# A state-space layer's skip, lows and carry moved between VectorE, TensorE, ScalarE and GpSimd

## The chip, the cores and the metric

One core of one Trainium2 chip runs the whole program in one launch. The metric is the device time of one execution in microseconds (us). Engines are named as in the profile: PE is TensorE's matmul side, PEld its weight loads, DVE is VectorE, ACT is ScalarE, POOL is GpSimd, SP issues the DMAs.

## The reference, cut to what matters

The program is two stacks of transformer-like layers over 256 tokens of width 1024. The change touches only the third layer of the first stack, a diagonal complex state space ("S5") with 64 groups of 64 states. With `u = xn @ w_in` it computes, in complex numbers, the recurrence `x[t] = a * x[t-1] + bbar @ u[t]`, and then

```
y = (einsum(c_re, xr) - einsum(c_im, xi))       # the outputs' sums
y = y.reshape(B, L, D_MODEL) + d_skip * u       # the skip
hg = gelu(y) @ w_glu
```

followed by a gated product and the residual. The layer is followed by a feed-forward layer and the rest of the program.

## The kernel before

All data are held feature-major: 128 partitions by 8 blocks of 256 tokens (`U5[:, k, :]` is `u` for block k). Weights stream from HBM in units of 1 MB into a ring of three; for every unit ACT makes the high part (L381, `whi`) and DVE the low part (L896, `wlo`), and PE multiplies high by high, high by low and low by high (L1683 to L1685). An operand has the same two parts: `XH` (ACT, counted by `op_hi`) and `XL` (DVE, counted by `op_lo`).

The order of work on each engine is written out by hand; every engine runs its own program in order and waits on semaphores. In the state space even and odd tokens are paired, so 128 pairs are scanned. They are cut in two halves of 64 (c = 0, 1) and the groups in four quarters (b = 0 to 3, called `qd` in places). That makes eight steps s = 2b + c. Steps of the two halves use two sets of four work buffers, `W5[s % 2]`. One step is:

- PE has written the inputs' sums of quarter b into banks 0 to 3 (L2206, `inputs(b)`, signalled by `bu_ready`).
- DVE, `products(s)`: four products of the sums in PSUM with tables in SBUF (L1317 to L1320), then an addition and a subtraction in SBUF (L1322, L1323).
- DVE, `scans(s)`: two scans (L1339, L1340). In the second half (c = 1) the state of the first half is first added in (L1337); it is computed after the first half's scans by four small products (L1346) and two small sums (L1353, L1354), on DVE ("jump"). Then two products turn the result back (L1348, L1349), signalled by `rot_ready`.
- POOL makes the two other products of the turn (L2406, L2407), signalled by `x5_ready`.
- PE, `outputs(s)`: 64 small fp32 products into bank 4 + b % 2 (L2235), signalled by `y5_ready`. With c = 0 the bank is zeroed first and a direct term is added (L2219, L2223). Between `outputs` PE computes one unit of an unrelated row of modulation vectors per step (L1697), and in odd steps the inputs of the next quarter ahead of it.
- DVE, `outputs(b)`: after both halves of quarter b, `u * d + sums` for its two blocks (L1362, `y5_sum`), put into DVE's queue after step 2b + 2. ACT then takes gelu (L664) and makes the high part (L666), and DVE makes the low part (`lows(b)`, L910), put after step 2b + 3.

After step 7 DVE makes the low part of a weight unit (L896), takes the sums of quarter 3 (L1362), copies the modulation rows (L984) and makes the last lows (L910). PE goes on with the gated product, whose first pass needs the lows of quarters 0 to 2 at once and those of quarter 3 after 18 matmuls.

A matmul of fp32 data stands in the trace as two records, a low-precision one as one.

Of the kernel before, what the change touches and what calls it, by code (L numbers as in the profile page):

```python
# [16 lines left out]
F32 = mybir.dt.float32  # L17
# [7 lines left out]
T = 256  # L25
# [43 lines left out]
def step5(s):  # L69

    return s % 2, s // 2
# [33 lines left out]
ITEMS, OUT0 = IN0 + 8, IN0 + 14  # L105

# [20 lines left out]
def program(nc, wst, mst, crow, vec, cst, xin, sgw, sgb, sbc, ctxin, ropes, out):  # L127
    with ExitStack() as ctx:
# [98 lines left out]
        def s5(i):  # L227
# [56 lines left out]
                 "v_ready", "scan_ready", "rot_ready", "x5_ready", "jump", "jump_parts", "y5_ready", "y5_sum",  # L284
                 "gelu5", "silu_c", "scp_nil", "mod_rows", "mod_sum", "mod_vec", "ctx_in", "mod_gain",
                 "c_in", "c_row", "ctx_rms", "ctx_inv", "ctx_diag", "ctx_row", "ml_in0", "ml_in1", "ml_used",
# [84 lines left out]
        def _(act):  # L371
# [275 lines left out]
            def state_space(i):  # L647
                scales()
                for n in range(4):
                    ahead(t.u)  # L650
                    t.u += 1
                    t.pp += 1
                    if n == 1:
                        turned(0)
                act.wait_ge(S["s5_k0"], 1)
                turned(1)
                act.activation(K0T, PS[:, 7, 0:256].rearrange("p (k n) -> p k n", n=32), ACT.Copy)\
                    .then_inc(S["s5_b"], 1)
                silu_c(1)
                t.u += MODS[0][1]  # L660
                for b in range(4):
                    act.wait_ge(S["y5_sum"], b + 1)
                    y = U5[:, 2 * b:2 * b + 2, :]
                    act.activation(y, y, ACT.Gelu_apprx_tanh).then_inc(S["gelu5"], 1)  # L664
                    act.wait_ge(S["gelu5"], b + 1)
                    act.activation(XH[:, 2 * b:2 * b + 2, T:2 * T], y, ACT.Copy).then_inc(S["op_hi"], 1)  # L666
                    if b == 2:
                        ahead(t.u)
                t.op += 4

                def ready(mp):
                    for j in (2 * mp, 2 * mp + 1):
                        ahead(t.u)
                        used(t.u)
                        act.activation(SG[:, j % 2, :], PS[:, 4 + t.pp % 2, T:2 * T], ACT.Sigmoid)\
                            .then_inc(S["glu_sig"], 1)
                        t.u += 1
                        t.pp += 1
                    act.wait_ge(S["glu_mul"], 2 * mp + 2)
                ahead(t.u)  # L680
                fresh(i, ready)
# [206 lines left out]
        def _(dve):  # L888
# [397 lines left out]
            def state_space(i):  # L1286
# [39 lines left out]
                def scans(s):  # L1326
# [16 lines left out]
                    if c == 0:  # L1343
                        zr, zi = (v.rearrange("p (a b) -> p a b", b=64)[:, :, 63] for v in (wk[1], wk[3]))
                        for o, x, y in ((JA, AR64, zr), (JB, AI64, zi), (JC, AR64, zi), (JD, AI64, zr)):
                            ins = dve.tensor_tensor(o[:, c8], x[:, c8], y, ALU.mult)  # L1346
                        ins.then_inc(S["jump_parts"], 1)
# [3 lines left out]
                    if c == 0:  # L1351
                        dve.wait_ge(S["jump_parts"], qd + 1)
                        dve.tensor_tensor(JRE[:, c8], JA[:, c8], JB[:, c8], ALU.subtract).then_inc(S["jump"], 1)  # L1353
                        dve.tensor_tensor(JIM[:, c8], JC[:, c8], JD[:, c8], ALU.add).then_inc(S["jump"], 1)  # L1354

                def outputs(b):

                    dve.wait_ge(S["y5_ready"], 2 * b + 2)
                    for kk in range(2):
                        u5 = U5[:, 2 * b + kk, :].rearrange("p (c e) -> p c e", e=2)  # L1360
                        y5 = PS[:, 4 + b % 2, kk * T:(kk + 1) * T].rearrange("p (e c) -> p c e", e=2)
                        ins = dve.scalar_tensor_tensor(u5, u5, vcol("ssm_d", 2 * b + kk), y5, ALU.mult, ALU.add)  # L1362
                    ins.then_inc(S["y5_sum"], 1)

                def lows(b):
                    low(XL[:, 2 * b:2 * b + 2, T:2 * T], U5[:, 2 * b:2 * b + 2, :], XH[:, 2 * b:2 * b + 2, T:2 * T],
                        t.op + b + 1)

                for s in range(8):
                    products(s)  # L1370
                    scans(s)
                    if s >= 2:
                        (lows if s % 2 else outputs)(s // 2 - 1)
                split_lo(t.s)
                t.s += 1
                outputs(3)
# [300 lines left out]
        def _(pe):  # L1677
# [505 lines left out]
            def state_space():  # L2183
# [26 lines left out]
                def outputs(s):  # L2210
# [5 lines left out]
                    if c == 0:  # L2216
                        if b >= 2:
                            pe.wait_ge(S["y5_sum"], b - 1)
                        pe.matmul(bank, ZB[:, 0:P], ZB[:, :], start=True, stop=False, **kw)  # L2219
                        for kk in range(2):  # L2220
                            for q in range(4):
                                r = slice(32 * q, 32 * q + 32)
                                pe.matmul(bank[r, kk * T:kk * T + P], K0T[r, 2 * b + kk, :], U5[r, 2 * b + kk, 0:T:2],  # L2223
                                          start=False, stop=False, **kw)
                    pe.wait_ge(S["rot_ready"], s + 1)
# [46 lines left out]
        def _(pool):  # L2272
# [127 lines left out]
            for s in range(8):  # L2400

                (c, qd), wk = step5(s), W5[s % 2]
                tc, ts = (AR[:, B0 + o + 512 * qd:B0 + o + 512 * qd + 512] for o in (12288, 10240))

                pool.wait_ge(S["rot_ready"], s + 1)
                pool.tensor_tensor(wk[1], wk[1], ts, ALU.mult)  # L2406
                pool.tensor_tensor(wk[3], wk[3], tc, ALU.mult).then_inc(S["x5_ready"], 1)  # L2407
# [109 lines left out]
```

## Time and profile before

| | us |
|---|---|
| three runs, median (lowest, highest) | 1827.54 (1827.36, 1828.07) |
| the profiled execution, its own time | 1829.06 |
| its span, first to last instruction | 1827.2 |
| PE busy | 1708.1 (93%) |
| DVE busy | 1248.8 (68%) |
| ACT busy | 844.6 (46%) |
| POOL busy | 163.0 (9%) |

The span is the time from the first to the last instruction; the execution's own time holds what lies around it. Busy time says how long an engine had an instruction in work. Start times below are counted from the span's start; the eight steps run from about 684 us to 759 us.

### The profile page before, as it was taken

To read this page: it belongs to the slowest core of one execution; us is meant where nothing else is said; L and a number is where in the kernel's file an instruction comes from. 1 tells how busy PE (TensorE), PEld (TensorE's weight loads), DVE (VectorE), ACT (ScalarE), POOL (GpSimd) and SP (SyncE) were. 2 spreads that over 40 slices of the span, in tenths; PEclk is the share of its full clock that TensorE was granted. 3 is DMA by queue.
4 is the path that set the end of the run, shared out by engine and by line. 5 is a ranking of instruction groups with operands and counts; after the bars stand their busy time and mean duration, and the time that the engine had idled before them with its cause. 6 is when DMAs were issued, how large, how long until landed. Compare 5 with 4: busy or idle time off the path is not lost.

```text
span 1827.2 us, 34733 instructions
## 1 busy us (share of the span) xinstructions
PE 1708.1 (93%) x14503; PEld 1616.3 (88%) x14514; DVE 1248.8 (68%) x1580; ACT 844.6 (46%) x962; POOL 163.0 (9%) x130
## 2 busy tenths in 40 slices
PE   6999999889899997799999999999979899999997
PEld 6979999889899985699999988999978579889997
DVE  5847777786877759767777774777774575664444
ACT  5355554546455530355545445555554533143333
POOL 1002000104910062200000101000000000000000
PEclk9999999999999999999999999999989999899999
DMA  7904545544455423444555761454432121035551
GB/s 299 333 1 162 190 178 184 184 162 152 150 181 184 164 91 117 163 162 162 182 184 181 270 252 47 179 191 168 183 111 93 69 93 70 24 138 184 184 184 69
DMA packets 40050, 286.50 MB, mean 157 GB/s; under 512 B 4576, under 2 KB 4576, under 8 KB 5664
## 3 DMA queue, kind: packets, MB, share of 16 engines
q1 hardware_dynamic: 39024, 280.99, 42.8%
q10 hardware_dynamic: 944, 4.33, 0.7%
q8 instruction: 63, 1.03, 0.2%
q14 instruction: 19, 0.16, 0.0%
HBM read 284.25 MB, written 1.05 MB: 156 GB/s over the span
## 4 chain that ended last, share of the span: by engine, by line
PE 64%; DVE 17%; ACT 9%; issue 6%; POOL 2%; DMA 1%; DVEq 0%; ACTq 0%; POOLq 0%; SPq 0%
PE PS L1683 19%; PE PS L1684 18%; PE PS L1685 18%; ACT whi L381 4%; DVE wlo L896 4%; DVE AR L1082 4%; ACT AR L486 1%; POOL AR L2389 1%; PE PS L1779 1%; DVE AR L1193 1%; DVE XL L940 1%; DVE AR L1190 1%; ACT AR L576 1%; ACT AR L578 1%; PE PS L2235 1%
## 5 line engine op out<-in xcount | busy, mean ns | idle before, releaser
L1683 PE MATMUL PS<-XH,whi 128*128 128x256 f32 (+1 forms) x2696 | 788.8, 293 | 45.0 <-DVE wlo L896 23.8
L1684 PE MATMUL PS<-XL,whi 128*128 128x256 f32 (+1 forms) x2696 | 780.2, 289 | 0.0
L1685 PE MATMUL PS<-XH,wlo 128*128 128x256 f32 (+1 forms) x2696 | 780.1, 289 | 0.0
L896 DVE TENSOR_TENSOR wlo<-raw,whi 128x2048 fp32r<-128x2048 f32 x240 | 558.9, 2331 | 187.7 <-ACT whi L381 187.6
L1683 PEld LDWEIGHTS PS<-XH,whi 128*128 128x128 f32 x2696 | 523.6, 194 | 58.1 <-issue 34.0
L1684 PEld LDWEIGHTS PS<-XL,whi 128*128 128x128 f32 x2696 | 524.1, 194 | 4.4 <-issue 0.2
L1685 PEld LDWEIGHTS PS<-XH,wlo 128*128 128x128 f32 x2696 | 523.7, 194 | 4.1
L381 ACT ACTIVATE whi<-raw 128x2048 fp32r<-128x2048 f32 x240 | 456.0, 1902 | 72.8 <-PE PS L1685 48.4
L1683 PE MATMUL PS<-HH,whi 128*128 128x256 f32 x880 | 251.8, 286 | 13.0 <-DVE HL L1102 8.5
L1685 PE MATMUL PS<-HH,wlo 128*128 128x256 f32 x880 | 251.0, 285 | 0.0
L1684 PE MATMUL PS<-HL,whi 128*128 128x256 f32 x880 | 250.8, 285 | 0.0
L1683 PEld LDWEIGHTS PS<-HH,whi 128*128 128x128 f32 x880 | 170.7, 194 | 14.8 <-DVE HL L1102 9.5
L1082 DVE SCALAR_TENSOR_TENSOR AR<-AR,VEC 128x255 f32<-128x255 f32 (+1 forms) x352 | 161.7, 501 | 15.4 <-ACT AR L486 4.7
L1684 PEld LDWEIGHTS PS<-HL,whi 128*128 128x128 f32 x880 | 170.6, 194 | 0.0
L1685 PEld LDWEIGHTS PS<-HH,wlo 128*128 128x128 f32 x880 | 170.5, 194 | 0.0
L489 ACT ACTIVATE AR<-AR 128x256 f32<-128x256 f32 x88 | 36.7, 418 | 268.4 <-DVE AR L1082 268.4
L2389 POOL TENSOR_TENSOR AR<-AR 128x512 f32<-128x512 f32 x24 | 56.0, 2335 | 916.3 <-ACT AR L435 916.2
L486 ACT ACTIVATE AR<-AR,VEC 128x256 f32<-128x256 f32 x176 | 95.6, 590 | 86.1 <-DVE AR L1068 86.1
L1068 DVE TENSOR_TENSOR AR<-PS,SM 128x512 f32<-128x512 f32 x88 | 60.7, 689 | 27.2 <-PE PS L1685 24.1
L1683 PE MATMUL PS<-whi,XH 128*128 128x256 f32 x256 | 74.1, 289 | 2.5 <-DVE XL L940 2.5
L1684 PE MATMUL PS<-wlo,XH 128*128 128x256 f32 x256 | 73.3, 286 | 0.0
L1685 PE MATMUL PS<-whi,XL 128*128 128x256 f32 x256 | 73.2, 286 | 0.0
(336 smaller groups left out, 1583.7 us busy)
## 6 DMA issues: line engine op xcount, KB each, us to landing
raw<-wst SPq DMA_DIRECT2D x248, 1024.0 KB, 4.8
AR<-mst SPq DMA_DIRECT2D x17, 1024.0 KB, 6.2
XT<-x_in SPq DMA_DIRECT2D x2, 512.0 KB, 6.0
AR<-crow ACTq DMA_DIRECT2D x2, 512.0 KB, 5.8
AR<-sbc ACTq DMA_DIRECT2D x1, 1024.0 KB, 6.6
AR<-ctxin ACTq DMA_DIRECT2D x1, 1024.0 KB, 5.8
y_out<-XT SPq DMA_DIRECT2D x1, 1024.0 KB, 3.9
AR<-sgw ACTq DMA_DIRECT2D x1, 512.0 KB, 3.7
```

The source lines that it names most:

```text
L381: act.activation(whi[:, r, :], raw[:, u % RING, :], ACT.Copy).then_inc(S["w_hi"], 1)
L486: a = act.activation(CA[:, j % 2, i, :], UA[:, j % 2, i, :], ACT.Identity, bias=cb, scale=w2)
L489: act.activation(SG[:, j % 2, :], CA[:, j % 2, 1, :], ACT.Silu).then_inc(S["silu_ready"], 1)
L576: act.activation(EX[:, p % 2, :], ZC[:, p % 2, :], ACT.Exp).then_inc(S["ex_ready"], 1)
L578: act.activation(LN[:, p % 2, :], EX[:, p % 2, :], ACT.Ln, bias=1.0)\
L896: dve.tensor_tensor(wlo[:, r, :], raw[:, u % RING, :], whi[:, r, :].bitcast(F32), ALU.subtract)\
L1068: dve.tensor_tensor(UA[:, j % 2], bank, RSTD.unsqueeze(1).broadcast_to([P, 2, T]), ALU.mult)\
L1082: ins = dve.scalar_tensor_tensor(y, UA[:, j % 2, i, 0:T - back], w, y, ALU.mult, ALU.add)
L1683: pe.matmul(dst, sh, mh, start=first, stop=False, **kw)
L1684: pe.matmul(dst, sh, ml, start=False, stop=False, **kw)
L1685: return pe.matmul(dst, sl, mh, start=False, stop=last, **kw)
L2389: ins = pool.tensor_tensor(SQ[:, 0:2, :], SQ[:, 0:2, :], SQ[:, 2 * mp:2 * mp + 2, :], ALU.add)
```

## The change

Four pieces of work of the eight steps move. (1) The skip: POOL multiplies `U5` by `d_skip` in place, two instructions per quarter, after the first half's `outputs` have been computed (`u5_skip`); PE adds the result into the bank with two fp32 matmuls by the identity, just ahead of the second half's `outputs`; DVE's L1362 is gone. (2) ACT takes its gelu straight from the PSUM bank when `y5_ready` says that both halves are there, and writes it to `U5`; the bank is released by `gelu5`. (3) The lows of quarters 0 to 2 are made by POOL; those of quarter 3 stay on DVE. (4) The four small products and two small sums that carry the state from the first half to the second are made by POOL, ahead of its two products of the turn.

```
 # ACT
-                    act.wait_ge(S["y5_sum"], b + 1)
+                    act.wait_ge(S["y5_ready"], 2 * b + 2)
                     y = U5[:, 2 * b:2 * b + 2, :]
-                    act.activation(y, y, ACT.Gelu_apprx_tanh).then_inc(S["gelu5"], 1)
+                    act.activation(y.rearrange("p k (c e) -> p k c e", e=2),
+                                   PS[:, 4 + b % 2, :].rearrange("p (k e c) -> p k c e", k=2, e=2), ACT.Gelu_apprx_tanh)\
+                        .then_inc(S["gelu5"], 1)
 # DVE, scans(s)
-                    if c == 0:
-                        zr, zi = (v.rearrange("p (a b) -> p a b", b=64)[:, :, 63] for v in (wk[1], wk[3]))
-                        for o, x, y in ((JA, AR64, zr), (JB, AI64, zi), (JC, AR64, zi), (JD, AI64, zr)):
-                            ins = dve.tensor_tensor(o[:, c8], x[:, c8], y, ALU.mult)
-                        ins.then_inc(S["jump_parts"], 1)
...
-                    if c == 0:
-                        dve.wait_ge(S["jump_parts"], qd + 1)
-                        dve.tensor_tensor(JRE[:, c8], JA[:, c8], JB[:, c8], ALU.subtract).then_inc(S["jump"], 1)
-                        dve.tensor_tensor(JIM[:, c8], JC[:, c8], JD[:, c8], ALU.add).then_inc(S["jump"], 1)
-
-                def outputs(b):
-
-                    dve.wait_ge(S["y5_ready"], 2 * b + 2)
-                    for kk in range(2):
...
-                        ins = dve.scalar_tensor_tensor(u5, u5, vcol("ssm_d", 2 * b + kk), y5, ALU.mult, ALU.add)
-                    ins.then_inc(S["y5_sum"], 1)
 
                 def lows(b):
+                    dve.wait_ge(S["op_lo"], t.op + b)
...
                 for s in range(8):
                     products(s)
                     scans(s)
-                    if s >= 2:
-                        (lows if s % 2 else outputs)(s // 2 - 1)
                 split_lo(t.s)
                 t.s += 1
-                outputs(3)
+                dve.wait_ge(S["y5_ready"], 8)
 # PE, outputs(s)
                         if b >= 2:
-                            pe.wait_ge(S["y5_sum"], b - 1)
+                            pe.wait_ge(S["gelu5"], b - 1)
...
+                    if c:
+                        pe.wait_ge(S["u5_skip"], b + 1)
+                        for kk in range(2):
+                            pe.matmul(bank[:, kk * T:(kk + 1) * T], ident,
+                                      U5[:, 2 * b + kk, :].rearrange("p (c e) -> p e c", e=2), start=False, stop=False, **kw)
                     pe.wait_ge(S["rot_ready"], s + 1)
 # POOL
+                for s in range(8):
+                    (c, qd), wk = step5(s), W5[s % 2]
...
+                    if c == 0:
+                        pool.wait_ge(S["scan_ready"], s + 1)
+                        zr, zi = (v.rearrange("p (a b) -> p a b", b=64)[:, :, 63] for v in (wk[1], wk[3]))
+                        for o, x, y in ((JA, AR64, zr), (JB, AI64, zi), (JC, AR64, zi), (JD, AI64, zr)):
+                            ins = pool.tensor_tensor(o[:, c8], x[:, c8], y, ALU.mult)
+                        ins.then_inc(S["jump_parts"], 1)
+                        pool.wait_ge(S["jump_parts"], qd + 1)
+                        pool.tensor_tensor(JRE[:, c8], JA[:, c8], JB[:, c8], ALU.subtract).then_inc(S["jump"], 1)
+                        pool.tensor_tensor(JIM[:, c8], JC[:, c8], JD[:, c8], ALU.add).then_inc(S["jump"], 1)
+                    pool.wait_ge(S["rot_ready"], s + 1)
+                    pool.tensor_tensor(wk[1], wk[1], ts, ALU.mult)
+                    pool.tensor_tensor(wk[3], wk[3], tc, ALU.mult).then_inc(S["x5_ready"], 1)
+                    b = s // 2
+                    if s % 2 == 0 and s:
+                        pool.wait_ge(S["op_hi"], OP5 + b)
+                        k = slice(2 * b - 2, 2 * b)
+                        pool.tensor_tensor(XL[:, k, T:2 * T], U5[:, k, :], XH[:, k, T:2 * T].bitcast(F32), ALU.subtract)\
+                            .then_inc(S["op_lo"], 1)
+                    if s % 2 == 0:
+                        pool.wait_ge(S["y5_ready"], s + 1)
+                        for kk in range(2):
+                            u5 = U5[:, 2 * b + kk, :]
+                            ins = pool.tensor_scalar(u5, u5, vcol("ssm_d", 2 * b + kk), None, ALU.mult)
+                        ins.then_inc(S["u5_skip"], 1)
```

## Rows read from the trace of the kernel before

**Rows 1.** Chain in order of time (start us, us, what): one round of two steps
```profile
699.95 0.69 DVE AR L1317
...
706.17 0.42 DVE SM L1346 x4
...
713.19 2.21 issue
```

**Rows 2.** Timeline of DVE (start us, us, instruction, [idle before <-releaser]), steps 2 to 4
```profile
706.51 0.68 DVE L1348 TENSOR_TENSOR AR<-AR 128x512 f32<-128x512 f32 x1
...
707.71 0.16 DVE L1353 TENSOR_TENSOR SM<-SM 128x8 f32<-128x8 f32 x1
...
707.86 0.87 DVE L1362 SCALAR_TENSOR_TENSOR AR<-AR,VEC,PS 128x256 f32<-128x256 f32 x2
...
708.65 0.68 DVE L1317 TENSOR_TENSOR AR<-PS,AR 128x512 f32<-128x512 f32 x1
...
711.16 0.69 DVE L1322 TENSOR_TENSOR AR<-AR 128x512 f32<-128x512 f32 x1
...
716.36 0.68 DVE L910 TENSOR_TENSOR XL<-AR,XH 128x512 fp32r<-128x512 f32 x1
717.40 0.69 DVE L1317 TENSOR_TENSOR AR<-PS,AR 128x512 f32<-128x512 f32 x1 [0.36 <-PE PS L2206]
```

**Rows 3.** Timeline of POOL, step 2
```profile
707.87 1.27 POOL L2406 TENSOR_TENSOR AR<-AR 128x512 f32<-128x512 f32 x1 [5.62 <-DVE AR L1349]
709.10 1.27 POOL L2407 TENSOR_TENSOR AR<-AR 128x512 f32<-128x512 f32 x1
```

**Rows 4.** Timeline of PE, from the inputs of quarter 2 to outputs(4)
```profile
717.29 2.99 PE L1697 MATMUL PS<-raw,SM 128*32 128x256 f32 x13
...
726.33 0.66 PE L2223 MATMUL PS<-AR,VEC 32*32 32x128 f32 x16 [0.25 <-DVE AR L1362]
727.97 1.99 PE L2235 MATMUL PS<-AR 128*32 128x64 f32 x128 [0.98 <-POOL AR L2407]
```

**Rows 5.** Timeline, POOL and DVE side by side, in the layer before
```profile
456.24 1.90 POOL L2304 COPY AR<-AR 128x2048 f32<-128x2048 f32 x1
```

**Rows 6.** Timeline of DVE in the layer before: L1102 beside L2304, and alone
```profile
456.78 1.90 DVE L1102 TENSOR_TENSOR HL<-AR,HH 128x512 fp32r<-128x512 f32 x1 [0.70 <-ACT HH L502]
...
474.89 0.73 DVE L1102 TENSOR_TENSOR HL<-AR,HH 128x512 fp32r<-128x512 f32 x1
```

**Rows 7.** Timeline behind step 7: POOL's turn beside DVE's weight lows, and outputs(7)
```profile
751.26 1.64 POOL L2406 TENSOR_TENSOR AR<-AR 128x512 f32<-128x512 f32 x1 [6.13 <-DVE AR L1349]
751.70 3.35 DVE L896 TENSOR_TENSOR wlo<-raw,whi 128x2048 fp32r<-128x2048 f32 x1
752.86 3.31 POOL L2407 TENSOR_TENSOR AR<-AR 128x512 f32<-128x512 f32 x1
...
756.32 3.15 PE L2235 MATMUL PS<-AR 128*32 128x64 f32 x128 [5.60 <-POOL AR L2407]
...
759.54 0.87 DVE L1362 SCALAR_TENSOR_TENSOR AR<-AR,VEC,PS 128x256 f32<-128x256 f32 x2 [4.49 <-PE PS L2235]
```

**Rows 8.** Timeline of POOL before the steps: prices of its operations
```profile
443.40 0.26 POOL L2296 TENSOR_TENSOR AR<-AR 128x32 f32<-128x32 f32 x1
...
674.47 0.60 POOL L2382 COPY AR<-AR 64x512 f32<-64x512 f32 x1
675.05 1.49 POOL L2383 TENSOR_SCALAR AR<-AR 64x512 f32<-64x512 f32 x1
```

**Rows 9.** Groups of instructions, PE: fp32 products with 256 moving columns
```profile
L1883 PE MATMUL PS<-AR,CST 128*128 128x256 f32 x32 | 11.4, 440 | 4.0 <-DVE AR L1193 3.8
```

**Rows 10.** Stretches: us, busy PE, PEld, DVE, ACT, POOL (count), PEclk, DMA share, GB/s
```profile
700.00:717.40 17.40, 13.93 (x369) 9.64 (x369) 16.80 (x31) 1.26 (x2) 5.63 (x5) 1.00 0.37 124
751.20:762.50 11.30, 5.49 (x146) 5.23 (x146) 6.05 (x7) 3.92 (x4) 4.92 (x2) 0.85 0.53 187
```

**Rows 11.** Timeline of PE: the gated product waits for the last lows
```profile
762.52 0.39 PE L1683 MATMUL PS<-XH,whi 128*128 128x256 f32 x1 [0.71 <-DVE XL L910]
```

More of the change, by code:

```diff
@@ L105 @@
 ITEMS, OUT0 = IN0 + 8, IN0 + 14
+OP5 = 6 * KT + 4
 class Tally:
@@ L283, in program @@
                  "s5_angle", "s5_table", "s5_xb", "s5_turned", "s5_b", "bu_ready", "bu_mult",
-                 "v_ready", "scan_ready", "rot_ready", "x5_ready", "jump", "jump_parts", "y5_ready", "y5_sum",
+                 "v_ready", "scan_ready", "rot_ready", "x5_ready", "jump", "jump_parts", "y5_ready",
                  "gelu5", "silu_c", "scp_nil", "mod_rows", "mod_sum", "mod_vec", "ctx_in", "mod_gain",
-                 "c_in", "c_row", "ctx_rms", "ctx_inv", "ctx_diag", "ctx_row", "ml_in0", "ml_in1", "ml_used",
+                 "c_in", "c_row", "u5_skip", "ctx_rms", "ctx_inv", "ctx_diag", "ctx_row", "ml_in0", "ml_in1", "ml_used",
                  "normed", "wide_taken", "csq", "csum", "crms", "crinv", "cnormed", "kv_part", "q_out", "rot",
@@ L1350, in scans @@
                         .then_inc(S["rot_ready"], 1)
-                    if c == 0:
-                        dve.wait_ge(S["jump_parts"], qd + 1)
-                        dve.tensor_tensor(JRE[:, c8], JA[:, c8], JB[:, c8], ALU.subtract).then_inc(S["jump"], 1)
-                        dve.tensor_tensor(JIM[:, c8], JC[:, c8], JD[:, c8], ALU.add).then_inc(S["jump"], 1)
-                def outputs(b):
-                    dve.wait_ge(S["y5_ready"], 2 * b + 2)
-                    for kk in range(2):
-                        u5 = U5[:, 2 * b + kk, :].rearrange("p (c e) -> p c e", e=2)
-                        y5 = PS[:, 4 + b % 2, kk * T:(kk + 1) * T].rearrange("p (e c) -> p c e", e=2)
-                        ins = dve.scalar_tensor_tensor(u5, u5, vcol("ssm_d", 2 * b + kk), y5, ALU.mult, ALU.add)
-                    ins.then_inc(S["y5_sum"], 1)
                 def lows(b):
+                    dve.wait_ge(S["op_lo"], t.op + b)
                     low(XL[:, 2 * b:2 * b + 2, T:2 * T], U5[:, 2 * b:2 * b + 2, :], XH[:, 2 * b:2 * b + 2, T:2 * T],
@@ L2399, in _, with turns @@
             shifted_outputs()
[L2400 to L2407, printed above, removed]
+            def turns():
+                for s in range(8):
+                    (c, qd), wk = step5(s), W5[s % 2]
+                    c8 = slice(8 * qd, 8 * qd + 8)
+                    tc, ts = (AR[:, B0 + o + 512 * qd:B0 + o + 512 * qd + 512] for o in (12288, 10240))
+                    if c == 0:
[22 more added lines that the diff above has]
+                        ins.then_inc(S["u5_skip"], 1)
@@ L2408, in _ @@
+            turns()
             for n in range(5, 8):
```

## The prediction

> **What bounds the kernel now.** I read the table of busy times first: PE is busy for 93% of the span, so a layer costs time mainly where PE stands still, and the eight steps of the state space are such a place. The stretches [rows 10] say who is full there: of 17.40 us DVE is busy 16.80, PE 13.93, POOL 5.63. Then the chain in order of time [rows 1], for one round of two steps: from step 2's first product (699.95) to step 4's (717.40, [rows 2]) is 17.45 us. It runs DVE (products, scans, the carry's small products L1346, turn), POOL (two products, 707.87 to 710.37 [rows 3]), PE's outputs, and the next quarter's inputs, with 2.21 us in the middle in which PE waits for nothing that the profile shows. The timeline of DVE [rows 2] shows that this is not alone: DVE's own work of the round fills all but 0.36 us before 717.40. And PE has 0.98 us left in a round [rows 4]. So three loops of nearly one length run side by side: DVE 17.1, POOL with PE 17.45, PE's own work some 16.5. Shortening one gives only the distance to the next. Last I read what follows step 7 [rows 7, 11].
>
> **What DVE loses in work.** Start to start in [rows 1, 2]: the four small products 0.34 (706.17 to 706.51), the two small sums 0.15 (707.71 to 707.86), the skip 0.79 (707.86 to 708.65), the lows 0.60 (0.68 long, the next starts 0.08 before its end). That is 1.88 a round: an even step is 7.91 - 0.49 = 7.42, an odd one stays at 7.71 (708.65 to 716.36), together 15.13. The 0.34 also lies on the chain through POOL.
>
> **What POOL gains, and its prices.** Six small products or sums of 128x8, one low part of 128x512, two scalings of 128x256. Small: 128x32 takes 0.26 and 128x512 takes 1.27 [rows 3, 8], so 2.1 ns an element and 0.20 for 8 elements, 0.16 start to start; bounds 0.15 and the 0.34 that a chained one needs with its wait (0.26 and 0.08 of handing on). Low part: 1.27, the same form as L2406. Scaling: the same operation on 512 elements of 64 partitions takes 1.49, a copy of that size 0.60 [rows 8]; half of each and a little start gives 0.8 and 0.4. I take 0.8, since the operation is the same, and keep both ends.
>
> **They exclude each other.** This decides the case. L2407 beside the weight lows L896 takes 3.31 instead of 1.27 [rows 3, 7]: L2406 ends at 752.90, L896 ends 2.15 later, L2407 1.12 after that. So L896 stood behind L2406 and L2407 behind L896. In [rows 5, 6] L2304 ends at 458.14 and L1102, 0.73 alone, ends at 458.68 after 1.90. Each time one ends its own length less 0.15 after the other's end, and they take turns. Beside products that read PSUM there is no such thing: L2406 and L2407 take 1.27 beside L1317 of step 3 [rows 2, 3]. Today POOL works almost only there. The new work doesn't: the small products start with DVE's turn (L1348), the low part and the scalings fall beside L1322, L1323, L1337 and the scans, all of them with two inputs in SBUF.
>
> The Trainium skill, SBUF — State Buffer, section Who interferes with whom, says the same as a rule: a VectorE instruction with two SBUF inputs contends with a GpSimd one that reads SBUF, whoever issues first gets the pair for the whole instruction, and the other fully blocks. The trace agrees for L896 and L1102; for the scans, which also have two, no run here shows it. By the rule they take part; without them the sum would be about 1.5 us less.
>
> **The round, with turns.** Let R be the end of DVE's turn in an even step. Two of the six small ones get between L1348 and L1349 and just behind; four are left, with a wait of POOL for its own count, so L2406 starts at R + 0.77 instead of R + 0.08. The chain through POOL becomes 17.45 - 0.34 + 0.69 = 17.8. L2407 ends at R + 3.27. DVE comes to L1322 at R + 2.44, so it ends 0.68 late; POOL's low part has the next turn, L1323 ends 1.05 late (its shift by 0.68 not counted again); PE's outputs end near R + 5.6 and the two scalings of 0.8 come beside L1337 and the scans, 0.6 each. Sum 2.93. DVE's loop is 15.13 + 2.93 = 18.06, the longest of the three: +0.61 against 17.45. So the work taken off DVE comes back as waiting, and a little more.
>
> **The skip on PE.** Two fp32 products by the identity: 32 records of mostly this form take 11.4 us busy [rows 9], 0.36 each, so about 0.71 a product as an upper bound; two records of 0.23 (13 of L1697 in 2.99, [rows 4]) give 0.46 as the lower. PE's own round is 6.8 (707.87 + 2.64 to 717.29) and 9.7 (717.29 to 726.99), 16.5; with 0.9 to 1.4 it is 17.4 to 17.9, under 18.06: hidden. Were DVE not the longest, PE would be. Its wait for `u5_skip` has the outputs and everything of PE behind it, but the scalings end some 5 us before PE gets there. The wait for `gelu5` in place of `y5_sum` is for a bank freed a round earlier: nothing.
>
> **Sum up to step 7.** Step 0 and 1: no low part, but L1322 is late by 0.68 and the scalings meet the turn of step 1, 1.04: +1.72 - 0.49, less a wait for PE that goes (I take the 0.36 of step 4) = +0.87. Steps 2 and 3: +0.61. From 717.40 to R of step 7, 751.18 ([rows 7], L2406's start less 0.08), it is 33.78 now; then 18.06 + 7.42 + 7.79 + 2.93 = 36.20: +2.42. This last is most of it, since no chain through PE stands beside DVE in steps 6 and 7. Together +3.9.
>
> **Behind step 7.** Now 751.18 to 756.17 for POOL's two products. Then DVE, rid of the low part, starts L896 (2.30 alone by [rows 7]) before POOL wakes: 2.22 + 1.12 + 1.23 = 4.57, -0.42. Next, outputs(7) takes 3.15 where the same takes 1.99 at full clock [rows 4, 7]: PE stood still for 5.60 us before and the granted clock of that stretch is 0.85 [rows 10]; PE will stand still nearly as long, so I keep it. ACT then starts on PSUM itself: L1362's 0.87 and its handing on go. But PE waits only 0.71 for the last lows [rows 11], behind 18 matmuls that it can do anyway, so that is all it gets: -0.71. Gelu from PSUM in another order may be slower than 0.63; this has 0.2 us of cover. Everything behind is bound by PE and shifts along.
>
> Total +3.9 - 0.42 - 0.71 = +2.8. The profiled execution, 1829.06 (span 1827.2), becomes 1831.8; the runs lie 1.5 below it, so 1827.54 + 2.8 = 1830.3, 0.15% more. What this kernel's measurement can tell from no change is about 0.2%, 3.7 us: 1823.9 to 1831.2.
>
> **Rivals.**
> (A) POOL's new work costs DVE nothing, because the scans don't take part and the short pieces slip into gaps. For it: small instructions, off DVE's queue, and DVE idles between its own waits. Against it: [rows 5 to 7]. Then PE's own work bounds the rounds (-0.2 up to step 6), steps 6 and 7 give DVE's 0.49 and 0.79, and the end 0.42 and 0.71: -2.6, 1824.9; with scalings and clock kinder still, 1823.5.
> (B) Slower: POOL's small work between scans and turn. If each of the six costs 0.34 instead of 0.16, L2406 starts 0.9 later still, all that follows on POOL meets more of DVE's scans, and four even steps pay 0.6 to 0.7 more each: 1830.3 + 2.8 = 1833.1. It decides from about 0.25 a piece. For it: every chained small one of the setup needs 0.34 with its wait, and the reads of the state have a stride of 64 elements, which no row shows. Against it: only one of six waits here.
> (C) PE is kept awake by the skip's products before outputs(7), which then takes 2.0: 1.2 less than the forecast, 1829.1. Against it: PE still stands still some 5 us.
> (D) Scalings cheap (0.4) and scans free of turns: the chain through POOL binds at +0.35 a round, and the end takes most of it back: 1827.8. The Trainium skill, GPSIMD Engine Reference, section 4.1 Engine selection, calls one-input work there roughly line-rate, which speaks for the cheap end, about 2 us less than my sum; the 1.49 of [rows 8] speaks against it.
>
> **Numbers.** Forecast 0.45, B 0.25, D 0.12, A 0.12, C 0.06. The forecast's own spread is 1.5 us, so a quarter of it is above 1831.2, with nine tenths of B: slower 0.34. Faster is the better half of A and what I haven't thought of: 0.10. The rest, 0.56, is no change. The range is 1824.8 (A's) to 1833.8 (a little over B's).
>
> **What would show it.** Right: L1322 of the odd steps at 1.3 to 1.4 us, L1323 at 1.7, scans of the odd steps at 1.8; POOL's low part at 1.7; L1322 to L1323 of even steps unchanged at 0.69; R of step 7 some 4 us later; the start of the gated product's seventh block 2 to 3 us later than 762.52 with no wait. Wrong: scans at 1.22 and 1.20 beside POOL's scalings (then D or A), R of step 7 earlier than 751.18 (A), small products at 0.3 (B), outputs(7) at 2 us (C), or PE's stall of 2.2 us in a round going away or coming twice, which would move a round by as much.

## The result and the profile after

| | before | after |
|---|---|---|
| median of 8 runs each (lowest, highest), us | 1827.45 (1825.42, 1830.30) | 1832.01 (1830.73, 1836.68) |
| the profiled execution: its own time, span | 1829.06, 1827.2 | 1831.81, 1829.7 |
| busy PE, DVE, ACT, POOL | 1708.1, 1248.8, 844.6, 163.0 | 1713.5, 1248.5, 844.6, 183.7 |
| steps: first product of step 0 to the gated product's first matmul | 683.96 to 759.40, 75.44 | 684.28 to 766.66, 82.38 |

The ratio after to before is 1.0033 [1.0021, 1.0044]: 0.33%, or 4.6 us in medians. That is slower by more than the 0.2% that this kernel's measurement can tell. The forecast was 1830.3 in a range of 1824.8 to 1833.8.

The steps cost 6.9 us more, the profiled span only 2.5. Up to the gated product everything is late by 7.26; the rest of the program, in which nothing was changed, took 4.8 us less in this pair of profiles, which hold one execution of each kernel. The section on the prediction comes back to it.

The busy times of the page after, against the table of before:

```profile
span 1829.7 us, 34778 instructions
...
PE 1713.5 (94%) x14530; PEld 1615.5 (88%) x14530; DVE 1248.5 (68%) x1545; ACT 844.6 (46%) x962; POOL 183.7 (10%) x165
```

DVE has lost 35 instructions (1580 before) and is busy as long as before: what it waits for within an instruction counts as busy. Its timeline after (start us, us, instruction, [idle before <-releaser]), step 3 and the start of step 4, to hold against [rows 2]:

```profile
708.50 0.68 DVE L1320 TENSOR_TENSOR AR<-PS,AR 128x512 f32<-128x512 f32 x1
...
711.01 1.42 DVE L1325 TENSOR_TENSOR AR<-AR 128x512 f32<-128x512 f32 x1
712.36 1.76 DVE L1326 TENSOR_TENSOR AR<-AR 128x512 f32<-128x512 f32 x1
...
714.43 1.22 DVE L1342 TENSOR_TENSOR_SCAN AR<-AR 128x512 f32<-128x512 f32 x1
715.58 1.35 DVE L1343 TENSOR_TENSOR_SCAN AR<-AR 128x512 f32<-128x512 f32 x1
716.96 0.78 DVE L1346 TENSOR_TENSOR AR<-AR 128x512 f32<-128x512 f32 x1
...
720.39 0.69 DVE L1320 TENSOR_TENSOR AR<-PS,AR 128x512 f32<-128x512 f32 x1 [2.04 <-PE PS L2190]
...
740.86 0.69 DVE L1320 TENSOR_TENSOR AR<-PS,AR 128x512 f32<-128x512 f32 x1 [3.10 <-PE PS L2190]
```

The addition and the subtraction (L1325, L1326; they were L1322 and L1323) take 1.42 and 1.76 instead of 0.69 and 0.68. And then DVE stands idle for 2.04 and 3.10 us until PE has the next inputs; before, that was 0.36 [rows 2]. The timeline of POOL after, same stretch, to hold against [rows 3]:

```profile
707.32 1.66 POOL L2399 TENSOR_TENSOR SM<-SM,AR 128x8 f32<-128x8 f32 x4 [3.60 <-DVE AR L1343]
...
709.39 1.28 POOL L2405 TENSOR_TENSOR AR<-AR 128x512 f32<-128x512 f32 x1
710.61 1.28 POOL L2406 TENSOR_TENSOR AR<-AR 128x512 f32<-128x512 f32 x1
711.84 1.73 POOL L2411 TENSOR_TENSOR XL<-AR,XH 128x512 fp32r<-128x512 f32 x1
714.40 3.25 POOL L2417 TENSOR_SCALAR AR<-AR,VEC 128x256 f32<-128x256 f32 x2 [0.83 <-PE PS L2224]
```

The low part (L2411) takes 1.73, and the two scalings 3.25 together beside the scans. The timeline of PE after, from step 2's modulation product to step 4's, answers to [rows 1, 4]:

```profile
707.21 3.62 PE L1681 MATMUL PS<-raw,SM 128*32 128x256 f32 x16
...
712.03 2.26 PE L2224 MATMUL PS<-AR 128*32 128x64 f32 x128 [0.30 <-POOL AR L2406]
714.22 0.49 PE L2190 MATMUL PS<-AR 32*128 32x128 f32 x3
717.69 2.65 PE L2190 MATMUL PS<-AR 32*128 32x128 f32 x61 [2.98 <-issue]
720.27 4.69 PE L1681 MATMUL PS<-raw,SM 128*32 128x256 f32 x16
724.89 1.17 PE L2212 MATMUL PS<-AR,CST 128*128 128x256 f32 x4
725.99 1.98 PE L2224 MATMUL PS<-AR 128*32 128x64 f32 x128
...
738.40 2.42 PE L2190 MATMUL PS<-AR 32*128 32x128 f32 x51 [3.49 <-issue]
```

Three things are to be seen. PE's wait for POOL ahead of outputs(2) has shrunk from about 1 us to 0.30. The gap inside the inputs (L2190; L2206 before), in which PE waits for nothing that the profile names, has grown from 2.21 to 2.98 and from 2.17 to 3.49. And behind it the same 16 records of modulation take 4.69 instead of 3.62. The stretches after (us, busy PE, PEld, DVE, ACT, POOL, PEclk, DMA share, GB/s) show the granted clock, against [rows 10]:

```profile
701.00:720.30 19.30, 16.02 (x374) 10.76 (x373) 17.11 (x22) 1.23 (x2) 14.01 (x16) 0.97 0.33 112
720.30:740.80 20.50, 17.01 (x376) 11.13 (x375) 16.93 (x22) 1.23 (x2) 11.99 (x14) 0.92 0.30 105
```

It was 1.00 in the round of before [rows 10]; after, it stands at the lower of its two levels (1.2 GHz instead of 2.4) for 3.4 us from 719.0 and again from 739.5, each time behind the long gap. PE's timeline of before has, for the second of its gaps:

```profile
733.02 1.63 PE L2206 MATMUL PS<-AR 32*128 32x128 f32 x43 [2.17 <-issue]
```

By rounds (first product of steps 0, 2, 4, 6, and the end of DVE's turn in step 7) it was 15.99, 17.45, 17.28, 16.49 before and is 16.59, 19.52, 20.47, 17.38 after. So the question of the experiments was what sets the two rounds of about 20 us: DVE's turn-taking with POOL, or PE's gap.

### The profile page after: what moved, and what is told of

The parts are those of the page before. It is cut to its first block, busy times and chain, and to the rows that moved or that the text cites. A ratio compares the mean times of both kernels' runs of the same rounds, so it can differ in the third digit from the quotient of the medians.

```text
span 1829.7 us, 34778 instructions
## 1 busy us (share of the span) xinstructions
PE 1713.5 (94%) x14530; PEld 1615.5 (88%) x14530; DVE 1248.5 (68%) x1545; ACT 844.6 (46%) x962; POOL 183.7 (10%) x165
## 4 chain that ended last, share of the span: by engine, by line
PE 66%; DVE 16%; ACT 9%; issue 6%; POOL 2%; DMA 1%; DVEq 0%; ACTq 0%; POOLq 0%; SPq 0%
PE PS L1667 19%; PE PS L1669 19%; PE PS L1668 19%; ACT whi L382 4%; DVE wlo L899 4%; DVE AR L1085 4%; ACT AR L487 1%; POOL AR L2378 1%; PE PS L2224 1%; PE PS L1763 1%; DVE AR L1196 1%; DVE AR L1193 1%; PE PS L1681 1%; ACT AR L577 1%; ACT AR L579 1%
```

## The experiments

Eleven kernels were run, in three groups, each beside the kernel before on its own chip (medians of before 1827.88, 1826.78 and 1827.95). "Steps" is the stretch of the table above; the gaps are the two inside PE's inputs; "rest" is from the gated product's start to the start of the last low part of a weight. Steps, gaps and rest are read from one profile of each kernel.

| kernel | median us | ratio to before | steps | gaps | rest |
|---|---|---|---|---|---|
| before | | 1 | 75.44 | 2.21, 2.17 | 1049.57 |
| after | 1832.01 | 1.0033 [1.0021, 1.0044] | 82.38 | 2.98, 3.49 | 1044.72 |
| e1_skip_only | 1833.42 | 1.0033 [1.0021, 1.0044] | 80.85 | 3.25, 3.52 | 1047.56 |
| e2_skip_back | 1828.92 | 1.0009 [0.9999, 1.0018] | 76.10 | 1.66, 1.80 | 1048.39 |
| e3_before_pad | 1830.87 | 1.0017 [1.0008, 1.0027] | 77.61 | see below | 1046.42 |
| e4_after_pad | 1835.34 | 1.0039 [1.0025, 1.0054] | 80.58 | see below | 1048.53 |
| e5_after_late | 1828.49 | 1.0008 [0.9999, 1.0018] | 78.12 | 1.06, 0.94 | 1044.70 |
| e6_after_split | 1835.60 | 1.0043 [1.0026, 1.0059] | 85.30 | 2.98, 3.41 | 1047.78 |
| e7_before_split | 1829.08 | 1.0011 [1.0001, 1.0021] | 79.35 | 2.48, 2.28 | 1047.74 |
| e8_act_split | 1832.49 | 1.0031 [1.0021, 1.0041] | 83.74 | 2.98, 2.78 | 1046.66 |
| e9_act_late | 1828.29 | 0.9996 [0.9986, 1.0006] | 74.14 | 1.48, 0.95 | 1048.13 |
| e10_before_late | 1824.87 | 0.9986 [0.9977, 0.9995] | 75.45 | 1.11, 0.83 | 1046.76 |
| e11_skip_late | 1825.13 | 0.9989 [0.9979, 0.9998] | 74.59 | 1.06, 1.16 | 1045.46 |

**First group: which part costs, and does the gap belong to a place in the program?**

e1_skip_only keeps the skip (parts 1 and 2) and puts the carry and the lows back on DVE:

```
+                    if c == 0:      # DVE, scans(s)
+                            ins = dve.tensor_tensor(o[:, c8], x[:, c8], y, ALU.mult)
...
+                    if s % 2 and s >= 3:
+                        lows(s // 2 - 1)
```

> Only the skip's part of the change: GpSimd scales, PE adds through the identity, ScalarE takes gelu from PSUM. The carry (four products, two sums) and all lows are on VectorE as before. Two theories. (P) PE's own loop has become the longest: the identity's products cost it 1.1 us a round and the gap inside the inputs (L2206) is longer than 2.2 us, because PE now comes to the burst without waiting. Then the rounds stay at 19 to 20 us, the steps (first product of step 0 to the first matmul of the gated product, 75.4 us before, 82.4 after) take 80 to 83, VectorE waits 2 us or more for L2206 in steps 4 and 6, and the time is 4 to 6 us over the kernel before. (T) The turns that VectorE and GpSimd take on each other (L1325 1.41, L1326 1.76 in the changed kernel) are the cost: then with no low part and no carry on GpSimd most of it goes, the steps take 75 to 77 us and the time is within 1 us of the kernel before.

Measured: the whole loss is there with the skip alone, 1.0033. PE's timeline shows the long gap and the slow stretch behind it, and DVE, whose work of a round is less than before by the skip, waits 2.81 and 3.88 us for the inputs:

```profile
717.76 2.89 PE L2200 MATMUL PS<-AR 32*128 32x128 f32 x61 [3.25 <-issue]
720.58 4.44 PE L1691 MATMUL PS<-raw,SM 128*32 128x256 f32 x16
724.95 1.17 PE L2222 MATMUL PS<-AR,CST 128*128 128x256 f32 x4
```

The second gap is 3.52. So PE's side sets the rounds, not the turn-taking.

e2_skip_back is the other half: carry and lows on POOL, the skip back on DVE, and gelu behind it as before.

```
+                        ins = dve.scalar_tensor_tensor(u5, u5, vcol("ssm_d", 2 * b + kk), y5, ALU.mult, ALU.add)
+                    ins.then_inc(S["y5_sum"], 1)
```

> The other half alone: the carry and the lows of quarters 0 to 2 stay on GpSimd, the skip is VectorE's sum as before, no identity products, no scaling, gelu from SBUF. (P): PE's program in the steps is that of the kernel before, so its gap stays at 2.2 us and its loop at some 17.3; VectorE's loop is 15.9 plus turns of 0.7 and 1.1, 17.7; the steps take 76 to 78 us and the time is 0 to 2 us over the kernel before. (T): the turns are the cost and are all here except the scalings': the steps take 80 us or more, the time 3 us or more over the kernel before.

Measured: 1.0009 [0.9999, 1.0018], steps +0.7. PE waits 1.4 us for POOL ahead of the even outputs, and the gaps are down to 1.66 and 1.80, where I had expected them to stay at 2.2. Waits and gap go against each other: outputs that start later come nearer to the moment at which the gap ends anyway.

e3_before_pad and e4_after_pad put products on 32x32 zeros into PE's program, without any use for them, so that new blocks of PE's program begin at other places in the work:

```
+                for _ in range(69):     # ahead of the steps; 65 in e4
+                    pe.matmul(PS[0:32, 6, 0:32], ZB[0:32, 0:32], ZB[0:32, 0:32], start=True, stop=True)
...
+                    for _ in range(59 if s == 7 else 0):     # 63 in e4
```

> The kernel before with 69 tiny padding products (138 instructions of PE) put where PE waits ahead of step 0, and 59 more where it waits ahead of outputs(7), 256 instructions in all, so that the program behind keeps its place in 16 KB blocks. If the gap of 2.2 us inside the inputs of quarters 2 and 3 is PE waiting for the next block of its program (16384-byte packets on the instruction queue start at 712.95 and 730.59, within 0.3 us of both gaps), the gap moves out of the inputs by 118 to 146 instructions, to the modulation products behind them or to another burst, and the rounds become VectorE's 17.1: the steps 0.5 to 1 us shorter. If the gap has to do with the data or the semaphores of the inputs it stays at the same matmul and nothing changes.

> The changed kernel with 65 such padding products ahead of step 0 and 63 ahead of outputs(7). (P) with the gap as a wait for the program: the gaps of 2.98 and 3.49 us leave the inputs, PE's loop falls from 19.5 and 20.5 to some 17, VectorE's loop with its turns (15.1 plus 2.1, 17.2) becomes the longest: the steps take 76 to 78 us instead of 82.4, the time comes back to within 1.5 us of the kernel before. (T): the turns don't change, so the steps stay above 80 us.

Both missed in time: the steps were 2.2 longer in e3 than in before and only 1.8 shorter in e4 than in after, and neither kernel was faster than the one it was made from. The 80.58 of e4 even lies where the rival (T) had it; the steps alone would not have told the two apart. What they did show is where the gap went. PE's timeline of e3:

```profile
722.80 1.77 PE L2235 MATMUL PS<-AR 128*32 128x64 f32 x113 [1.05 <-POOL AR L2411]
728.65 0.65 PE L2235 MATMUL PS<-AR 128*32 128x64 f32 x15 [4.09 <-issue]
```

and of e4:

```profile
723.91 1.75 PE L2224 MATMUL PS<-AR 128*32 128x64 f32 x109
729.85 0.74 PE L2224 MATMUL PS<-AR 128*32 128x63 f32 x18 [4.20 <-issue]
```

The gap has left the inputs and stands within outputs(3), and is longer: 4.09 and 4.20. It follows the position in PE's program and not the work, which speaks for the fetch of the program. In the packets of e3 the weight load lies at 722.89 to 726.48 and the program's packet starts at 726.44; in e4 the load ends at 727.55 and the packet starts at 727.55. That gave the next theory: the block is fetched only when the weight load that is under way ends.

**Second group: the load in the way of the block.** In the kernel before, the DMA rows of 709.50 to 712.90 show the 1 MB load alone on queue q1:

```profile
DMA packets 132, 1.05 MB, mean 308 GB/s; under 512 B 4, under 2 KB 4, under 8 KB 4
...
q1 hardware_dynamic: 132, 1.05, 88.2%
```

and those of 709.50 to 713.90 have one packet more of queue q8, 16 KB of instructions, which starts at 712.95:

```profile
DMA packets 145, 1.07 MB, mean 242 GB/s; under 512 B 16, under 2 KB 16, under 8 KB 16
...
q1 hardware_dynamic: 144, 1.05, 68.3%
q8 instruction: 1, 0.02, 1.3%
```

After, the load lies at 711.97 to 715.44 and 732.56 to 736.09, and the packets start at 715.44 and 736.09. The load is issued 1.15 us behind the even step's modulation product, which frees its buffer. So from the end of that product to PE's going on there is a nearly fixed time: 708.60 to 715.40 and 726.08 to 733.02 before, 710.83 to 717.69 and 731.42 to 738.40 after; 6.80, 6.94, 6.86, 6.98. In e1 it is 6.89 and 7.00, in e2 6.60 and 6.97. It is the 1.15 to the load, 3.4 to 3.5 of the load, and 2.25 to 2.45 from the packet's start to PE's next matmul.

The Trainium skill, Runtime: NRT & Kernel Launch, section Instruction fetch mechanics, says that an engine's program comes in blocks of 256 instructions while the present one runs, and that crossing a boundary is mostly hidden. The blocks agree with the 16 KB packets here; the hiding does not: PE stands for 1.7 to 4.2 us in the kernels up to e4.

e5_after_late changes nothing but the time of two loads: in `load` SP also waits until PE has the inputs of the round. (For this SP's loop over these loads is written out, as it is in e6 to e11 too.)

```
                 sp.wait_ge(S["w_used"], before + 1 + step)
+                if before - MODS[0][0] in (2, 4):
+                    sp.wait_ge(S["bu_ready"], (before - MODS[0][0]) // 2 + 2)
```

> The changed kernel, PE's program untouched; only SP issues two of the weight loads later: those that fill the place of the modulation units 2 and 4 also wait until the inputs of quarters 2 and 3 are computed. New theory (Q): in every run so far the program block that PE lacks in its gap starts on the DMA engines exactly when the 1 MB weight load ends (before: loads end at 713.15 and 730.71, blocks start at 712.95 and 730.59; changed: 715.44 and 736.09, blocks at 715.44 and 736.09), and PE goes on 2.3 us later. The load starts 1.15 us after the modulation product of an even step, so the inputs end at a fixed time after that product and PE's 1 us of waiting ahead of outputs(2) was never to spare. With the loads out of the way the block comes within a few tenths of PE's reaching the one before: the gaps inside the inputs (2.98, 3.49) fall under 0.7 us, the rounds from 19.5 and 20.5 to 17.2 to 18.5, and a shorter gap may come in the outputs of steps 3 and 5, beside the moved loads. Rival (R): the gap is the time that a block always takes, the load only happens to end then: gaps and rounds stay.

Measured: steps 78.12 instead of 82.38, 1.0008 instead of 1.0033. With no load near (the loads lie at 706.81 to 710.36 and 720.21 to 727.20), the DMA rows of 710.80 to 715.80 hold the block alone, at 714.71:

```profile
DMA packets 1, 0.02 MB, mean 3 GB/s; under 512 B 0, under 2 KB 0, under 8 KB 0
...
q8 instruction: 1, 0.02, 1.3%
```

and the timeline of PE has short gaps and no slow stretch behind them:

```profile
717.06 2.09 PE L2192 MATMUL PS<-AR 32*128 32x128 f32 x61 [1.06 <-issue]
719.08 3.64 PE L1683 MATMUL PS<-raw,SM 128*32 128x256 f32 x16
...
734.24 1.85 PE L2192 MATMUL PS<-AR 32*128 32x128 f32 x51 [0.94 <-issue]
```

DVE's turn-taking is untouched by this, as its timeline says:

```profile
712.28 1.42 DVE L1327 TENSOR_TENSOR AR<-AR 128x512 f32<-128x512 f32 x1
713.62 1.76 DVE L1328 TENSOR_TENSOR AR<-AR 128x512 f32<-128x512 f32 x1
```

With no load near, the packet starts 1.41 us behind the first product of outputs(2) and again of outputs(4) (713.30 and 730.52 in e5); in after it was 3.41 and 3.83, in before 2.43 and 2.62. This settles the cause of the long rounds: the load delays the block, and the delay closes PE's loop. The gaps stayed a little over the 0.7 that I had expected. The rounds from steps 2 and 4 fell from 19.52 and 20.47 to 17.23 and 17.35; the first round is longer than in after, 17.75 instead of 16.59, with the granted clock at the lower level for 10.2 us from 691.2 instead of 6.8 from 691.7.

e6_after_split and e7_before_split cut these loads into four of 256 KB, so that the block could come between them:

```
+                    for c0 in range(512, UNIT, 512):
+                        sp.dma_start(raw[:, u % RING, c0 - 512:c0], wst[u][:, c0 - 512:c0]).then_inc(S[f"piece{u % RING}"], 16)
```

> The changed kernel with each of the five weight loads between two modulation units issued as four DMAs of 256 KB (512 columns each) instead of one of 1 MB. (Q), if the block waits in its DMA engines for the rest of one transfer: it gets in between the pieces, the gaps shrink by some 2 us to about 1, rounds 17.5 to 18.5, steps 77 to 79 us. If it waits for all that is queued, split or not, the gaps stay at 3.0 and 3.5 and so does the time.

> The kernel before with the same split loads. (Q): its gaps of 2.21 and 2.17 go or shrink below 1; the chain through PE gets shorter than VectorE's own loop of 17.1, so the rounds fall only from 17.45 and 17.28 to 17.1: 0.5 us in all, not to be seen in the time.

Missed. The pieces of the loads between two steps together take 5.4 to 5.9 us in e6 instead of 3.45. The block does start within the load there (716.82, in a load of 713.41 to 718.88, and 737.43, in one of 733.59 to 739.49), but not sooner: 3.37 and 3.85 us behind the first product of the outputs, with whole loads 3.41 and 3.83. The gaps are 2.98 and 3.41, and in e7 2.48 and 2.28. Both kernels have SP's loop written out and still have the gaps, so it was not this that shortened them in e5. PE's timeline of e6 has the slow stretch in the inputs themselves, 3.42 for 61 records:

```profile
719.15 3.42 PE L2197 MATMUL PS<-AR 32*128 32x128 f32 x61 [2.98 <-issue]
```

e8_act_split has the split loads, carry and lows on DVE, and the scaling on ACT instead of POOL:

```
+                        a = act.activation(u5, u5, ACT.Copy, scale=vcol("ssm_d", 2 * b + kk))
+                    a.then_inc(S["u5_skip"], 1)
```

> A version that should beat both if (Q) holds: the skip through the identity with its scaling on ScalarE instead of GpSimd (so GpSimd and VectorE never meet), gelu from PSUM, carry and lows on VectorE as before, split loads. VectorE's loop is 17.1 less 0.8 for the skip's sums, 16.3; PE's 16.5 less 2.2 for the gap plus 1.1 for the identity, 15.4; through GpSimd 17.45 less 2.2. Rounds of 16.3 to 16.6, steps 72 to 73 us against 75.4 before, time 2 to 4 us under the kernel before. If splitting doesn't shorten the gap, PE's loop of 19.5 stays and it is as slow as the skip alone, 80.9 us of steps.

Missed too, and twice: the gaps are 2.98 and 2.78 and the rounds from steps 2 and 4 20.02 and 19.06; and there is a new wait in quarter 3, where the scaling stands in ACT's queue behind the high parts of weights. PE's timeline:

```profile
761.66 2.07 PE L2234 MATMUL PS<-AR,CST 128*128 128x256 f32 x4 [7.64 <-ACT AR L671]
```

**Third group: late loads in every version.** e9 is e8 with the loads whole and late, e10 the kernel before with late loads, e11 the skip alone (e1) with them. Each has the lines of e5:

```
+                if before - MODS[0][0] in (2, 4):
+                    sp.wait_ge(S["bu_ready"], (before - MODS[0][0]) // 2 + 2)
```

> The version that both findings point to: the skip through the identity, scaled on ScalarE (quarter 3's scaling ahead of the weight highs that come between gelu 2 and 3), gelu from PSUM, carry and lows on VectorE, and the two weight loads held until the inputs are computed. (Q): gaps of about 1 us or less, no turns on VectorE; VectorE's loop 16.3, PE's 16.5 - 2.2 + 1.0 + 1.1 = 16.4; rounds of 16.3 to 16.7, steps 72.5 to 74 us against 75.4 before, time 1.5 to 3 us under the kernel before (ratio 0.9985 to 0.999). (T), turns alone matter: also good, since there are none. (R), the gap doesn't depend on the load: rounds stay at 19.

> The kernel before with the two held loads alone. (Q): the gaps of 2.21 and 2.17 fall to 1 or less, but VectorE's own loop of 17.1 takes over at once: rounds 17.1 to 17.2, the time within 1 us of the kernel before. So what e9 gains over this is the skip's.

> The skip alone with its scaling on GpSimd (as in the changed kernel), carry and lows on VectorE, held loads. Against e9 it shows what the scalings' turns cost: VectorE's loop 16.2 plus 0.3 for scans and turn that start late, so rounds of 16.4 to 16.8; against the skip alone with early loads (rounds 19.8 and 20.5, 1.0033) it shows what the load costs: some 3 us a round. Time within 1 us of e9. If GpSimd's scalings push its own products of the odd step late, up to 17.2.

e9 can't be told from before; e10 and e11 are below it, by 0.14% [0.05, 0.23] and 0.11% [0.02, 0.21], less than the 0.2% that I called the bound. They beat both kernels of the case in their medians, though little, and are not to be told from each other. The gaps and rounds came out nearly as expected (16.3 to 16.8 in e9, 16.5 and 16.8 in e11, 17.0 in e10), the times did not: e9 gained nothing of its 1.5 to 3 us, and e10, which was to gain at most 1, gained most. PE's timeline of e11 shows the round without its stall:

```profile
715.85 2.09 PE L2202 MATMUL PS<-AR 32*128 32x128 f32 x61 [1.06 <-issue]
...
732.62 1.85 PE L2202 MATMUL PS<-AR 32*128 32x128 f32 x51 [1.16 <-issue]
```

Two differences can be read from the group. e1 to e11, with the skip: holding the loads takes 6.3 us off the steps. e11 to e5, both with late loads: the steps with carry and lows on POOL are 78.12 - 74.59 = 3.5 us longer, but 1.5 of that lies in the first round, where the clock of e5 was lower for longer; the other rounds are longer by 0.5, 0.8 and 1.5, and what follows step 7 is 0.7 shorter. Here DVE is the longest again, and the turn-taking is what one pays. In e10 the steps are as long as before (75.45) although both gaps halved, because PE now waits for POOL instead (1.64 us ahead of outputs(4)); its gain in the median lies outside the steps, and its cause was not settled:

```profile
715.86 1.96 PE L2208 MATMUL PS<-AR 32*128 32x128 f32 x57 [1.11 <-issue]
729.13 2.03 PE L2237 MATMUL PS<-AR 128*32 128x64 f32 x128 [1.64 <-POOL AR L2409]
```

So of what e5 and e11 gain in time over after and e1, up to some 2.6 us may be this same gain and not the shorter gaps; no run has SP's loop written out with nothing else changed.

## Why the prediction was right or wrong

The direction was right and the time within 1.7 us, but the class was not: I gave "no change" 0.56 and it is slower. And the mechanism was half of the real one; that the time came so near is in part luck, since the stretch with the change lost more than twice the forecast and the rest of the program, which the forecast left as it was, took less. Up to the gated product's seventh block I forecast +2.8; it starts at 769.22 instead of 762.52 [rows 11], +6.4 us when the start of step 0 (+0.3) is taken off. The rounds say where the 3.6 us of error are: steps 0 and 1 +0.60 (forecast +0.87), steps 2 and 3 +2.07 (+0.61), from there to the end of step 7's turn 37.85 instead of 33.77, +4.08 (+2.42), and behind that -0.37 (-1.13).

**The step that failed** is "The skip on PE", where it said "PE's own round is 6.8 ... and 9.7 ..., 16.5; with 0.9 to 1.4 it is 17.4 to 17.9, under 18.06: hidden". The working counted PE's 0.98 us ahead of outputs(4) [rows 4] as slack. It was none: the gap in the inputs ends about 6.9 us behind the even step's modulation product, whatever outputs do in between; outputs that start earlier only lengthen the gap. PE's loop was already 17.6 us (715.40 to 733.02: 10.7 of work from the inputs' going on to the end of the modulation product, 6.9 behind it), as long as the round. What is added to the 10.7 is added to the round: the identity products 1.10 (inside my 0.9 to 1.4), and, since the gap then grows and the clock falls behind it, 1.07 on L1681 and 0.6 on the inputs. 17.6 + 2.8 = 20.4, and the round from step 4 is 20.47; the one from step 2, in which the first long gap falls and whose start it doesn't yet set, is 19.52. I had listed the stall as something that might go or come twice; I had not asked what it hung on. e1, e5 and e11 together show this.

**Turn-taking on DVE.** Right in kind, and well in size for the additions: L1325 1.42 and L1326 1.76 (forecast 1.3 to 1.4 and 1.7), the low part 1.73 (1.7), POOL's turn 0.81 behind the end of DVE's (0.77). The Trainium skill's rule (SBUF — State Buffer, section Who interferes with whom), that the one who is behind fully blocks, agrees with the 1.42 and 1.76. Wrong for the scans: 1.22 and 1.35 where I had 1.8 each. There POOL waits, 3.25 for two scalings that take 0.93 each with nothing of DVE beside them (e4, at 739.43), and the scan hardly does. The first scaling starts at 714.40, the scan at 714.43; by that rule, in which the first one keeps the shared pair for its whole instruction, the scan should have waited as the additions did, and the measurement decides. DVE's cost of a round was thus 0.73 + 1.08 + 0.15 + 0.09 = 2.05 and not 2.93 (in step 5 it is 1.85). In the kernel as it was changed this is hidden, since DVE is idle for 2.04 and 3.10 us behind it; with the loads held it is part of what e5 has over e11.

**Small operations on POOL.** Forecast 0.20 each, measured 0.20 (L2402, L2403). Rival B, which had 0.34 for them, came out at nearly the right time (1833.1) for a wrong reason.

**Behind step 7.** POOL's two products 4.54 us by the forecast 4.57, right. The timeline of POOL after, against [rows 7]:

```profile
758.32 3.24 POOL L2405 TENSOR_TENSOR AR<-AR 128x512 f32<-128x512 f32 x1 [0.78 <-DVE AR L1347]
761.52 1.26 POOL L2406 TENSOR_TENSOR AR<-AR 128x512 f32<-128x512 f32 x1
```

The last lows are no longer waited for, as said (-0.71). But outputs(7) takes 3.81, not the 3.15 that I kept: the term is short by 0.66. The granted clock is at its lower level from 763.4 to 766.8, nearly all of outputs(7); before, it was from 755.4 to 758.8, with outputs(7) from 756.32 to 759.47.

**Rivals.** A (no cost on DVE) fell with L1325 and L1326. D was half right: the scans are nearly free of turns, 1.22 and 1.35, but the scalings are not cheap, 0.93 alone where D has 0.4 and the forecast 0.8, and its 1827.8 is missed by 4.2 because PE's loop binds. C (outputs(7) at 2 us) fell with its 3.81. The true rival, PE's loop as the longest, stands in the working as one clause without a price of its own.

**What the rest gave back.** Behind the steps the same code took 1044.72 instead of 1049.57. The clock's records there show 37.7 us at the lower level after and 47.8 before; over the thirteen kernels that time lies between 37.7 and 53.4 and the rest between 1044.7 and 1049.6. The shortest rests (after, e5, e11) have the least of it (37.7, 37.7, 41.9), but beyond these the order is loose: e2, with the most, is 1.2 us shorter than before. That the clock makes these differences is not shown, and one profile stands for each kernel. In medians the loss is 4.6 of the 6.9 us.

## What to carry to other kernels

A gap named "issue" inside a burst of small matmuls is a resource with its own loop: find out what its end is tied to (here the end of a weight load that the burst's own predecessor sets off) before counting a wait ahead of it as slack. A wait that grows shorter when the work in front of it comes later is no cover for new work. And work moved from DVE to GpSimd came back on DVE as waiting beside its additions with two inputs in SBUF, hardly beside the scans, and not beside products that read PSUM.

## What the runs showed of the hardware

- A 16 KB block of PE's program mostly comes only when a 1 MB load of another queue that is under way ends: it started within 0.2 us of the load's end in before (712.95, 730.59; loads to 713.15, 730.71) and at it in after (715.44, 736.09). It is not without exception. Of the blocks that start during a load that stands alone, or within 0.3 us of its end, 15 of 18 in the trace of before and 18 of 18 in that of after start in its last 0.5 us or behind it; in before the one of 722.19 starts at the load's beginning (722.10 to 726.09) and in e2 the one of 724.97 within it (723.02 to 727.70), and these loads take 3.99 and 4.68 instead of 3.45. Even with no load near, 0.83 to 1.48 us of gap are left (e5, e9 to e11).
- Cutting the load into four makes it longer, 5.4 to 5.9 us instead of 3.45 in e6, and doesn't help the block (gaps 2.98, 3.41). The Trainium skill, DMA: Bandwidth & Descriptors, section Queues, rings and completion order, has each DMA engine go round its queues packet by packet, with some 9 to 17 descriptors to such a packet and 64 at most. A whole load is 144 packets of the profile here; if each of them is one descriptor and they are spread evenly, which no run shows, that is 9 to an engine, an estimate, and a whole load can be one packet of the page. Blocks that start at the load's end agree with this, and so do the ones of e6 within split loads; that splitting brings nothing does not follow from it.
- The clock fell to its lower level behind the gaps of 2.98 and 3.49 us in the inputs (after), 3.25 and 3.52 (e1), and not behind 2.21 and 2.17 (before); 16 records of modulation then took 4.69 (after) or 4.44 (e1) instead of 3.62. The length of the gap doesn't decide it alone: in e7 it fell with gaps of 2.48 and 2.28, in e8 not with one of 2.78.
- GpSimd beside an addition with two SBUF inputs delays it by its own turn (0.69 to 1.42); beside a scan it is mostly GpSimd that waits (a scaling of 0.93 takes 1.3 to 1.9), and the scan takes 1.22 to 1.44 instead of 1.20 to 1.23.
